# One hybrid backbone layer on one core: a scan level's two directions in one PSUM bank with one masked copy, and the second norm turned in a new order and split over two engines

## What is computed

```python
h  = rmsnorm(x, g1) * (1 + sc1) + sh1
aq, ai, aff, afb, ag, bq, bk, bv, ga, gb = split_columns(h @ w_in)
o_a, s_f, s_b = hgrn2_mixer(aq, ai, aff, afb, ag, ...)     # gated linear recurrence, both directions
o_b = attention(bq, bk, bv, cached context, sink)          # window of 128 for latent tokens
y = (sigmoid(ga) * (o_a @ w_oa) + sigmoid(gb) * (o_b @ w_ob)) @ w_out
x = x + gt1 * y
h2 = rmsnorm(x, g2) * (1 + sc2) + sh2
x = x + gt2 * peer(h2, p_wq, p_keys, p_u, p_v)             # 8 heads x 16 experts a token, looked up
```

## Time and profile before

| | us |
|---|---|
| median of 3 runs | 2622.94 (2609.85 to 2630.68) |
| profiled execution | 2617.25 |
| its span | 2615.4 |
| VectorE busy | 1734.0 (66%) |
| TensorE matmuls busy | 2019.9 (77%) |
| ScalarE busy | 972.8 (37%) |
| GpSimd busy | 936.7 (36%) |
| masked copies, L1516 | 75 of 0.73, 54.6 |
| table loads of ScalarE for gelu, L903 | 94 of 1.28, 120.6 |

### The profile page before, as it was taken

One profiled execution on the slowest core, in us unless ns is written; L12 is line 12 of the kernel. 1 busy time (PEld: TensorE's weight loads), 2 busy tenths in 40 slices (PEclk: granted clock), 3 DMA queues, 4 the chain that ended last, 5 costly groups with the idle time before them and its releaser, 6 DMA issues. The chain is left out here.

```text
span 2615.4 us, 27311 instructions
## 1 busy us (share of the span) xinstructions
PE 2019.9 (77%) x6925; PEld 1109.9 (42%) x6925; DVE 1734.0 (66%) x3917; ACT 972.8 (37%) x2489; POOL 936.7 (36%) x806
## 2 busy tenths in 40 slices
PE   6978897856666798787499786887867778787776
PEld 2667745745555533375255222322223222232222
DVE  3632278776766688728588677777776767776664
ACT  1412144353333334312433344444444434344443
POOL 0020022542222223203132564556555545454454
PEclk9998999978888899888699999999999999899999
DMA  8835678841121488858588999999999999999997
GB/s 321 287 137 179 228 292 309 302 162 65 65 81 49 192 329 346 314 200 328 194 349 335 401 421 397 412 422 422 421 408 412 421 391 404 388 414 417 392 418 296
DMA packets 113319, 805.69 MB, mean 308 GB/s; under 512 B 12596, under 2 KB 14006, under 8 KB 17046
## 3 DMA queue, kind: packets, MB, share of 16 engines
q0 software_dynamic: 93760, 680.96, 65.0%
q1 hardware_dynamic: 17704, 118.17, 12.3%
q10 hardware_dynamic: 1712, 4.98, 0.5%
HBM read 800.79 MB, written 3.28 MB: 307 GB/s over the span
## 5 line engine op out<-in xcount | busy, mean ns | idle before, releaser
L1131 POOL DMA_INDIRECT RG<-in_uv,idxs x264 | 346.0, 1311 | 522.9 <-DVE pl L1382 280.5
L903 ACT ACTIVATE agel<-apre 128x1 f32<-128x1 f32 x640 | 129.1, 202 | 957.6 <-DVE apre L1354 952.9
L559 PE MATMUL pl<-RG,BP 128*128 128x512 f32 x576 | 295.0, 638 | 106.8 <-ACT BP L919 106.0
L559 PE MATMUL pl<-RING,BP 128*128 128x512 f32 x576 | 289.6, 637 | 77.8 <-ACT BP L919 76.1
L584 PE MATMUL pa<-HL,RING 128*128 128x512 f32 (+2 forms) x960 | 317.6, 489 | 9.8 <-DVEq L416 6.5
L1354 DVE CUSTOM_DVE_ANT_0 R<-RG,AB 128x1024 f32<-128x1024 f32 x201 | 246.2, 1228 | 98.8 <-DMA RG<-in_uv,idxs 78.7
L1131 POOL DMA_INDIRECT RING<-in_uv,idxs x168 | 230.3, 1371 | 208.3 <-PE pl L559 134.7
L1354 DVE CUSTOM_DVE_ANT_0 R<-RING,AB 128x1024 f32<-128x1024 f32 x168 | 206.0, 1226 | 113.6 <-DMA RING<-in_uv,idxs 73.7
L584 PEld LDWEIGHTS pa<-HL,RING 128*128 128x128 f32 x960 | 167.5, 198 | 152.2 <-issue 118.4
L559 PEld LDWEIGHTS pl<-RG,BP 128*128 128x128 f32 x576 | 100.5, 193 | 293.5 <-ACT BP L919 218.8
L559 PEld LDWEIGHTS pl<-RING,BP 128*128 128x128 f32 x576 | 108.3, 200 | 253.1 <-ACT BP L919 156.5
(11 more groups left out here) (256 smaller groups left out, 3187.3 us busy)
## 6 DMA issues: line engine op xcount, KB each, us to landing
RING<-in_in_slabs SPq DMA_DIRECT2D x42, 1024.0 KB, 5.0
RING<-in_pq_slabs SPq DMA_DIRECT2D x24, 1152.0 KB, 6.0
RING<-in_ada_slabs SPq DMA_DIRECT2D x16, 1024.0 KB, 5.2
RING<-in_out_slabs SPq DMA_DIRECT2D x12, 1024.0 KB, 4.8
RG<-in_col_slabs POOLq DMA_DIRECT2D x8, 1024.0 KB, 7.0
RING<-in_o_slabs SPq DMA_DIRECT2D x8, 1024.0 KB, 6.0
RG<-in_uv,idxs POOLq DMA_INDIRECT x297, 12.3
RING<-in_uv,idxs POOLq DMA_INDIRECT x168, 14.6
```

Source lines behind the costliest of these rows:

```text
L559: last = nc.tensor.matmul(acc[:, c * 512:(c + 1) * 512], DG[:, k % 2, :], bufs[k % len(bufs)][:, D + c * 512:D + (c + 1) * 512], start=Fal ...
L903: A(agel[:, par, k:k + 1], apre[:, par, k:k + 1], ACT.Gelu).then_inc(gel_done, 1)
L1131: nc.gpsimd.indirect_dma_start(out=bufs[b], out_offset=None, in_=uv, in_offset=bass.IndirectOffsetOnAxis(ap=idxs[:, par, k:k + 1], axis=0) ...
```

## The change

Scans:
- One group a level, `("lvl", u, l)`, in one bank. Direction 0 fills the columns whose bit l is 1 and direction 1 those whose bit is 0, so each of the eight matmuls has 64 moving columns, taken and written in pieces of 2^l. TensorE waits for both directions' updates ahead of it.
- VectorE and GpSimd both wait for that one group. VectorE makes one masked copy a level. The masks are 8 instead of 15.
- `settle` puts a slot that would stand ahead of a level behind the whole level; a level has one share of slots instead of two.

Second norm:
- The sum of squares follows the last add of its tile. One root instruction takes all tiles of the batch. Two tiles are scaled ahead.
- Order of the transposes: x2T of the next tile ahead of h2 of this one (`turn_order`).
- Of the eight copies ScalarE makes the first four and VectorE the last four, as `tensor_scalar` with two scalars a partition; TensorE waits for both.
- The shares of x2T and h2 in the planner's last stage fall from 4.0 to 2.5.

```diff
-          ("post2", 64, {"y": 3.4, "x2T": 4.0, "h2": 4.0, "qp": 5.2, "ss": 1.2}))
+          ("post2", 64, {"y": 3.4, "x2T": 2.5, "h2": 2.5, "qp": 5.2, "ss": 1.2}))
+def turn_order(tiles):
+
+    order = []
+    for i in range(len(tiles) + 1):
+        order.extend([("x2T", tiles[i])] if i < len(tiles) else [])
+        order.extend([("h2", tiles[i - 1])] if i else [])
+    return order
-            names.extend(("lvl", u, l, d) for d in range(2))
+            names.append(("lvl", u, l))
-        if nxt[0] == "lvl" and nxt[3] == 0:
+        if nxt[0] == "lvl":
             return at + 1
@@ TensorE, scan
+            def half(x, l, d):
+                return x.rearrange("p (n a i) -> p n a i", a=2, i=1 << l)[:, :, 1 - d, :]
                 for l in range(LEVELS):
                     for d in range(2):
                         pe.wait_ge(hg_ready[d], (LEVELS + 1) * u + l + 1)
-                        ps = start(("lvl", u, l, d))
-                        for b in range(4):
-                            last = mm(ps[:, bl[b]], HK[d][:, bl[b]], HQ[d][:, bl[b]])
-                        finish(("lvl", u, l, d), last)
+                    ps = start(("lvl", u, l))
+                    for b in range(4):
+                        for d in range(2):
+                            last = mm(half(ps[:, bl[b]], l, d), HK[d][:, bl[b]], half(HQ[d][:, bl[b]], l, d))
+                    finish(("lvl", u, l), last)
                     beat(u, l)
@@ ScalarE, post
-                for i, t in enumerate(tiles):
-                    beside.before(("x2T", t))
-                    root(NT + t)
-                    act.wait_ge(am_ready, 3)
-                    turned("x2T", t, 1, h2T_ready)
+                beside.before(("x2T", lo))
+                act.wait_ge(ssq_ready, NT + hi)
+                step(A(st[:, 16 + lo:16 + hi], st[:, 8 + lo:8 + hi], ACT.Sqrt), *[rms_ready] * len(tiles))
+                act.wait_ge(am_ready, 3)
+                for name, t in turn_order(tiles):
+                    ps = group((name, t))
+                    if name == "x2T":
+                        for k in range(KD // 2):
+                            step(A(h_tile(t, k), ps[:, k * P:(k + 1) * P], ACT.Identity,
+                                   scale=AM[:, 1, min(t, 1), k:k + 1], bias=ADA[:, 2, min(t, 1), k:k + 1]))
@@ GpSimd, scan
-                    beside.before(("lvl", u, l, 1))
-                    wait_full(pool, ("lvl", u, l, 1))
+                    beside.before(("lvl", u, l))
+                    wait_full(pool, ("lvl", u, l))
                     for ins in half_update(1, l, mul, u):
                         step(ins)
@@ VectorE, scan
-                    group(("lvl", u, l, 0))
+                    group(("lvl", u, l))
                     for ins in half_update(0, l, mul, u):
                         step(ins)
                     dve.sem_inc(hg_ready[0], 1)
-                    take(("lvl", u, l, 0), l)
-                    take(("lvl", u, l, 1), 7 + l)
+                    take(("lvl", u, l), l)
@@ VectorE, post
-                for t in tiles:
-                    ssq(X1[t], t, SQ2[b])
+                        if q == 3:
+                            ssq(X1[t], t, SQ2[b])
+                beside.before(("x2T", tiles[0]))
+                for t in tiles[:2]:
+                    normed(NT + t, X1[t], xn2(t))
                 for i, t in enumerate(tiles):
-                    beside.before(("x2T", t))
                     if i > 1:
-                        wait_full(dve, ("x2T", t - 2))
-                    normed(NT + t, X1[t], xn2(t))
+                        beside.before(("x2T", t))
+                        normed(NT + t, X1[t], xn2(t))
+                    ps = group(("x2T", t))
+                    for k in range(KD // 2, KD):
+                        step(V.tensor_scalar(h_tile(t, k), ps[:, k * P:(k + 1) * P], AM[:, 1, min(t, 1), k:k + 1],
+                                             ADA[:, 2, min(t, 1), k:k + 1], ALU.mult, ALU.add))
@@ masks
-        masks[:, l] = same & ((s >> l) % 2 == 0) & ((t >> l) % 2 == 1)
-        masks[:, 7 + l] = same & ((s >> l) % 2 == 1) & ((t >> l) % 2 == 0)
+        masks[:, l] = same & ((s >> l) % 2 != (t >> l) % 2)
```

47 lines of the change are left out of this document (25 added, 22 removed).

## The result

The changed kernel takes 2633.3 us, the kernel before 2622.9 (medians of 11 runs each): a ratio of 1.0042, interval 1.0026 to 1.0058. It is slower by 0.4%, where 1.2% less was forecast. Within 1% of before had a chance of 0.42; the median lies 13 us above the range (2565 to 2620).

The account below looks back on a forecast made before the run. A chain of waits, not an engine, paces the latent scans; the last batch's second norm is emptiest. Latent scans -9, unit 0 +2, batches 0 and 1 -4, batch 2 -20.5: -31.5 us, forecast 2590 us, range 2565 to 2620.

Parts of the forecast that it names:

- The view of what bounds the kernel: Latent scans: no engine is full, a chain of waits sets the pace; one beat closes in 6.14 us.
- the chain, 1.20 + 1.23 + 1.79 + 1.91: Latent beat: TensorE's first direction, VectorE's update, two masked copies, TensorE's turned probabilities and values; sum 6.13 us.
- The level matmuls: Scans: sixteen half-column matmuls take 1.20 us a level, about what eight whole ones take; 0.85 more kept for the range.
- the common wait: Scans: both updates start on one semaphore and collide, +0.7 us on VectorE's update and +0.4 on GpSimd's.
- The rival at 0.11: Scans: half-column matmuls cost whole ones, +0.85 us on 35 levels, +30 us, 2620 us; chance 0.11.
- Full exclusion: Scans: VectorE's and GpSimd's updates alternate operation by operation; +17 us against the forecast, 2607 us; chance 0.11.
- The slots: Latent scans: six beats with slots between VectorE's two copies lose about 1.8 us each, -11 us.
- The masks at nothing: Masks: conversion and transfer shrink but gain nothing, as VectorE idles 22.86 us for ScalarE; uncovered, about half a microsecond.
- Batches 0 and 1: Second norm: ScalarE does four copies instead of eight, VectorE the others; -1.95 us each batch, -4 together.
- Batch 2's norm: Last batch's second norm: first query 24.8 us earlier; -20.5 us after payback, from -27 to -6.
- 4 to pay back in the queries: Last batch's queries: they take over one expert pair and two slots' gathers, costing 4 us of the norm's gain.
- the bound of 0.5 each: Second norm, batches 0 and 1: VectorE's copies, put at 0.35 us each, would matter only above 0.5.

Follow-up runs that it names:

- two_waits: The changed kernel with the waits of before: half columns, one bank and one masked copy stay; 2582.4 us, ratio 0.9868 to the kernel before.
- sync_only: The kernel before with only its waits made common to both directions; whole columns, two banks, two masked copies; 2711.0 us, ratio 1.0369.
- slots_only: The kernel before with only the planner's new rule, slots behind both directions of a level; 2621.5 us, ratio 0.9997.
- norm_only: The kernel before with the norm's part of the change alone, scans as before; 2593.6 us, ratio 0.9907.
- the four norm kernels: norm_only, and it with all copies on ScalarE (2601.9 us), with the old transpose order (2597.6), or with both (2606.3).

## Why the prediction failed

*The view of what bounds the kernel* was right for a beat at the full clock: the chain, 1.20 + 1.23 + 1.79 + 1.91, held, and taking one copy out gave 0.95 us a beat in two_waits.

Two steps failed, the price of the level matmuls and the common wait. *The level matmuls* ("Sixty-four f32 columns move in half of the 0.117 us ... I take 1.20") failed. The rate was read from bf16 weight loads; an f32 instruction with 64 columns takes what one with 128 takes (2.00 and 2.05 for sixteen). The rival at 0.11 had this mechanism and its size, 0.85 a level: beats at the full clock are 6.65, where 6.03 + 0.85 = 6.9 follow. Against it I set a row of another type; whole f32 instructions with a load each were in rows 2 and 3.

*The common wait* was priced by its collision alone (+0.7 and +0.4), and this part held: 1.78 us for VectorE and 2.02 for GpSimd, on average of the latent beats (forecast 1.8 and 2.1 for the three operations). Full exclusion would have made some 2.2 for the one and 2.8 for the other (1.08 and 1.70 laid end to end are 2.8; the 2.5 of the prediction is too low); the rule of the Trainium skill (SBUF — State Buffer, "Who interferes with whom") was not borne out in full. What was missing is what TensorE does meanwhile: it stands 2.2 us where it stood 0.99, and the clock that it then gets. The earlier trace rows gave 0.83 for the scans, and 0.62 for the norm with its many pauses: both levels stood there to be read. With the waits alone changed the latent scans grew by 72 us in sync_only, the largest single effect of the study, of which some 34 (28 beats at 1.2) are the expectation's price at the full clock.

*The slots* (-11) failed: slots_only measured none. The beats shrank about as priced and the time came back elsewhere: behind the beat at 651 by the slow clock on the longer work that follows the shorter pause. Whether that is the whole of it stays open. A pause priced by its length alone was the error.

*The masks at nothing* was not tested by itself; nothing in the runs speaks against it. *Batches 0 and 1* (-4, by the split) is not shown: batch 0's stretch is as long in norm_only as before, and batch 1's 5 us also appear in kernels with the old norm.

*Batch 2's norm* held in sum: 23.1 us in norm_only, 24.4 in the changed kernel, 24.8 forecast with 4 to pay back in the queries, where norm_only shows nothing paid back (125.5 us from the first query to the last, as before). (24.8 less 4 is 20.8; the prediction writes 20.5.) That the size came out is in part luck, since its steps held less: I put the gain on hidden copies and slots, and 19 us were in what the four norm kernels share: the single root, the norms ahead, the early sums and the shares. VectorE's copies from PSUM take 1.75 us for four, not 1.4, under the bound of 0.5 each.

*What was not in the sum* is the tail: -18. The forecast had no step that changes where VectorE's loops lie, and the trace of before has the four stalls. Without these 18 us, which are luck, the changed kernel would lie near 2651.

With the measured sizes: latent scans +45, unit 0 +17, up to the latent scans -7, batch 1 -7, batch 2 -24, tail -18, in all +6.

## What to carry to other kernels

Price a merged wait by what the third engine does meanwhile. Where TensorE lives in a chain of short bursts, a longer pause costs twice, once as a pause and once as the low clock behind it; where narrower instructions save no time, as these with a weight load each, keep them as wide as they can be, since the narrow ones also lowered the clock. In a program with loops as long as this one (305 instructions), look for waits on nothing at the first instruction behind a backward jump before and after any edit ahead of it, and don't credit the edit with that difference: here it was 18 us, more than the 10 by which the whole change came out slower.

## What was unexpected of the hardware

- Sixteen f32 matmul instructions, each with its own weight load of 128 columns, take 2.00 and 2.05 us at 2.4 GHz with 64 and 128 moving columns, and 3.65 at 1.2 GHz with 64.
- At equal counts and waits, TensorE's clock in unit 0 was 0.56 with 64 moving columns and 0.98 with 128 for half of them.
- Twelve matmul instructions of no use in each pause brought a level from 6 us to 4.33.
- A backward jump of VectorE's loop of 305 instructions costs 4.6 to 5.5 us or nothing, by where the loop begins, and 2.9 to 3.5 more where it begins at 79 to 86; 48 semaphore increments 1400 us earlier decide it.
